# Two of six modulation vectors computed inside the recurrence instead of in the input stream

## The reference, cut to what matters

```python
def ada_modulation(cvec, w_mod, b_mod):
    m = jax.nn.silu(cvec) @ w_mod + b_mod          # (2 vectors, 2048) @ (2048, 6 * 2048)
    return jnp.split(m[:, None, :], N_MOD, axis=-1)

sh1, sc1, g1, sh2, sc2, g2 = ada_modulation(cvec, lp['w_mod'], lp['b_mod'])
h = rmsnorm(x, lp['n1']) * (1.0 + sc1) + sh1
(q, k, v, glu_a, glu_b, r, kc, vc, ...) = split_columns(h @ lp['w_in'])
# attention (q, k, v), convolution module (glu_a, glu_b), two-way RWKV-7 recurrence (r, kc, vc, ...)
y = jnp.concatenate([y_a, y_b, y_c], axis=-1) @ lp['w_out']
x = x + g1 * y
h2 = rmsnorm(x, lp['n2']) * (1.0 + sc2) + sh2
x = x + g2 * conv_ffn(h2, lp['w_up'], lp['ffn_conv_w'], lp['ffn_conv_b'], lp['w_down'])
```

## Time and profile before

| | us |
|---|---|
| median of 3 runs | 2195.0 (2190.41 to 2195.76) |
| the profiled execution, its own time | 2199.24 |
| its span | 2197.5 |
| PE busy in it | 2081.4 |
| DVE busy | 1042.3 |
| ACT busy | 725.4 |

### The profile page before, as it was taken

One profiled execution on the slowest core, in us unless ns is written; L12 is line 12 of the kernel. 1 busy time (PEld: TensorE's weight loads), 2 busy tenths in 40 slices (PEclk: granted clock), 3 DMA queues, 4 the chain that ended last, 5 costly groups with the idle time before them and its releaser, 6 DMA issues.

```text
span 2197.5 us, 43948 instructions
## 1 busy us (share of the span) xinstructions
PE 2081.4 (95%) x19367; PEld 1828.7 (83%) x19367; DVE 1042.3 (47%) x1821; ACT 725.4 (33%) x1224; POOL 169.5 (8%) x275
## 2 busy tenths in 40 slices
PE   6999999999888899899799999999999999999997
PEld 3578888777567787778699999999999998887886
DVE  2333223664657777543644444444443444445444
ACT  3231222222554444323433223333223333333433
POOL 1000000000325444200000000000000000000000
PEclk8999999999889999999899999999999999999999
DMA  9988767775310000163343343333434336333431
GB/s 370 370 289 295 291 250 276 279 267 201 97 31 9 18 16 14 61 267 115 134 135 127 122 135 117 133 127 123 134 117 132 129 121 249 126 124 115 134 134 58
DMA packets 204847, 343.01 MB, mean 156 GB/s; under 512 B 14782, under 2 KB 138484, under 8 KB 202545
## 3 DMA queue, kind: packets, MB, share of 16 engines
q1 hardware_dynamic: 203264, 335.15, 43.9%
q0 software_dynamic: 1392, 5.05, 0.7%
HBM read 332.62 MB, written 10.31 MB: 156 GB/s over the span
## 4 chain that ended last, share of the span: by engine, by line
PE 85%; DVE 8%; DMA 3%; issue 2%; POOL 1%; ACT 1%; SPq 0%; DVEq 0%; POOLq 0%; ACTq 0%
PE ps L812 25%; PE ps L814 24%; PE ps L813 24%; PE ps L851 3%; DMA ring<-in_w_mod_dram 3%; PE ps L1056 1%; PE ps L1048 1%; PE ps L1050 1%; PE ps L1173 1%; PE ps L1066 1%; POOL w_mix L690 1%; PE ps L1137 0%; PE ps L1106 0%; PE ps L998 0%; DVE h_split L1744 0%
## 5 line engine op out<-in xcount | busy, mean ns | idle before, releaser
L1675 DVE TENSOR_TENSOR w_split<-ring,w_split 128x1024 fp32r<-128x1024 f32 x392 | 474.6, 1218 | 715.8 <-ACT w_split L1348 715.5
L1348 ACT ACTIVATE w_split<-ring 128x1024 fp32r<-128x1024 f32 x392 | 406.7, 1051 | 845.7 <-PE ps L814 572.8
L812 PE MATMUL ps<-h_split,w_split 128*128 128x384 f32 x1776 | 597.6, 336 | 3.8 <-DVE h_split L2092 3.8
L813 PE MATMUL ps<-h_split,w_split 128*128 128x384 f32 x1776 | 594.5, 335 | 0.0
L814 PE MATMUL ps<-h_split,w_split 128*128 128x384 f32 x1776 | 594.4, 335 | 0.0
L812 PEld LDWEIGHTS ps<-h_split,w_split 128*128 128x128 f32 x1776 | 334.1, 188 | 14.9 <-issue 13.6
L813 PEld LDWEIGHTS ps<-h_split,w_split 128*128 128x128 f32 x1776 | 334.2, 188 | 0.0
L814 PEld LDWEIGHTS ps<-h_split,w_split 128*128 128x128 f32 x1776 | 334.2, 188 | 0.0
L812 PE MATMUL ps<-w_split,h_split 128*128 128x512 f32 (+1 forms) x528 | 201.7, 382 | 2.2 <-DVE w_split L1675 2.0
L813 PE MATMUL ps<-w_split,h_split 128*128 128x512 f32 (+1 forms) x528 | 197.4, 374 | 0.0
L814 PE MATMUL ps<-w_split,h_split 128*128 128x512 f32 (+1 forms) x528 | 197.4, 374 | 0.0
(11 more groups left out here) (370 smaller groups left out, 2503.5 us busy)
## 6 DMA issues: line engine op xcount, KB each, us to landing
ring<-in_w_up_dram SPq DMA_DIRECT2D x88, 1024.0 KB, 4.9
ring<-in_w_mod_dram SPq DMA_DIRECT2D x64, 1024.0 KB, 7.4
ring<-in_w_in_dram SPq DMA_DIRECT2D x46, 1024.0 KB, 5.4
ring<-in_w_down_dram SPq DMA_DIRECT2D x44, 1024.0 KB, 5.3
ring<-in_w_mod_dram SPq DMA_DIRECT2D x64, 512.0 KB, 7.0
ring<-in_w_out_dram SPq DMA_DIRECT2D x16, 1024.0 KB, 5.5
arena<-in_x_sample_dram SPq DMA_DIRECT2D x4, 1024.0 KB, 9.1
x_mid<-arena SPq DMA_DIRECT2D x1, 3072.0 KB, 10.0
```

The costliest lines, as they stand in the source:

```text
L812: mm(o_, lh, rh, start=start, stop=False)
L813: mm(o_, lh, rl, start=False, stop=False)
L1348: AC(wh[k % SPLITS][:, 0:width(n)], arrived(n), ACT.Copy).then_inc(s_hi, 1)
L1675: V.tensor_tensor(wl[k % SPLITS][:, 0:w], arrived(n), wh[k % SPLITS][:, 0:w].bitcast(F32), ALU.subtract).then_inc(s_lo, 1)
```

## The change

The stream keeps only sh2 and sc2 behind the early blocks: 4 late blocks instead of 8, so 32 pieces of 1 MB leave it. The gates' 32 MB come as 128 loads of 256 KB (one K-tile by 512 columns) into four slots in `h_f32`, of which only two are used from load 72 on. PE multiplies one such tile ("gate step", four products side by side in 128 columns each) ahead of steps that `gate_fill` names: 8 steps in each of the periods -1 to 14. A burst of 8 steps adds up in the upper half of bank 7; ACT copies it to `gpart`, POOL adds the two bursts of a block, SP writes the sum to DRAM. The gates' bias enters as one more product. F2's tile moves to the lower half of bank 7.

```diff
-N_MOD = 6 * D // MOD_W
+N_LATE = 2 * D // MOD_W
+N_MOD = 2 * D // MOD_W + N_LATE
+LATE_COL = N_LATE // 2
...
+GATE_W = 4 * P
+N_GATE = 2 * D // GATE_W
+GATE_STEPS = N_GATE * KT
+GATE_BANK = 7
+def gate_fill(u, step):
+    if u < 0:
+        return dict(cum=4, tr=4).get(step, 0)
+    if u == 0:
+        return dict(X0=2, lora=1, X1=1, T1=2, X2=2).get(step, 0)
+    return dict(ZU=2, lora=1, X1=1, T1=2, S0=2).get(step, 0)
+GATE_BURST = KT // 2
+def gate_done(u):
+    return sum(1 for w in GATE_PLAN if w <= u)
+GATE_WIDE = gate_done(NG + 1) // 4 * 4
+def gate_slot(n):
+    return n % 4 if n < GATE_WIDE else 2 + n % 2
...
+        gslot = [hf[:, TOK * k:TOK * k + GATE_W] for k in (12, KT + 12)]
+        gslot += [hf[:, TOK * k - GATE_W:TOK * k] for k in (KT, 2 * KT)]
+        gpart, grow = (hf[:, TOK * k:TOK * k + 2 * P].rearrange("p (i c) -> p i c", i=2) for k in (14, KT + 14))
@@ SP
+            def gate_loads(upto):
+                for n in range(gates_at[0], min(upto, GATE_STEPS)):
+                    i, q = divmod(n, KT)
+                    if i and q == KT // 2:
+                        gate_out(i - 1)
+                        gates_at[1] = i
+                    earlier = [m for m in range(n) if gate_slot(m) == gate_slot(n)]
+                    if earlier:
+                        sp.wait_ge(s_gu, earlier[-1] + 1)
...
+                    sp.dma_start(gslot[gate_slot(n)], a["w_mod"][0][P * q:P * q + P, c0:c0 + GATE_W]).then_inc(s_w[gate_slot(n)], 16)
             sp.wait_ge(s_blk, P_OUT)
+            gate_loads(4)
             bias_rows(sp, 1)
...
             for gr in range(GROUPS):
+                gate_loads(gate_done(NG * gr + 2))
                 sp.wait_ge(s_stc, gr + 1)
...
                 if gr == 0:
+                    gate_loads(gate_done(NG + 1))
                     sp.wait_ge(s_rbon, NG)
                     sp.wait_ge(s_rlora, NG)
                     sp.wait_ge(s_fy, 3)
                     sp.wait_ge(s_fg, 3)
                     for i in range(3):
                         if i:
+                            gate_loads(gate_done(NG + 1 + i))
                             sp.wait_ge(s_rlora, NG + 3 + i)
                         params(2, range(3 * i, 3 * i + 3))
                 if gr == 1:
+                    gate_loads(GATE_STEPS)
+                    for i in range(gates_at[1], N_GATE):
+                        gate_out(i)
@@ POOL
-            pool.wait_ge(s_grow, 1)
-            for i in range(2):
-                for g in range(2):
-                    pool.dma_start(G_dram[i, g].rearrange("(k p) -> k p", p=P), grow[g:2 * KT:2, i, :]).then_inc(s_G, 16)
...
+                if u >= 0 and u % 2 == 0 and u < 2 * N_GATE:
+                    i = u // 2
+                    pool.wait_ge(s_gev, 2 * i + 2)
...
+                    pool_tt(grow[:, i % 2, :], gpart[:, 0, :], gpart[:, 1, :], ALU.add).then_inc(s_gsum, 1)
@@ PE
-            for i, c0 in enumerate((2 * KT, 5 * KT)):
-                last = tr(ps[0:2 * KT, 4, toks(i)], modcol[:, c0:c0 + KT, :].rearrange("p k g -> p (k g)"), ident)
-            last.then_inc(s_gT, 1)
+            own_bank = dict(F1=0, F2=0, out=0)
+            own_bank["in"] = 0
+            def gate_step(k):
+                for n in range(gates_at[0], min(gates_at[0] + k, GATE_STEPS)):
...
+                    first = n % GATE_BURST == 0
+                    if first and n:
+                        pe.wait_ge(s_gev, n // GATE_BURST)
+                    for taken, count in ((s_fc, own_bank["F2"]), (s_stc, own_bank["out"]), (s_S0, 2 * own_bank["in"])):
+                        if count:
+                            pe.wait_ge(taken, count)
+                    pe.wait_ge(s_w[gate_slot(n)], gate_landed(n))
+                    at = [ps[32 * g:32 * g + 2, GATE_BANK, HW:HW + P] for g in range(MG)]
+                    if q == 0:
+                        for g in range(MG):
+                            mm(at[g], modcol[:, tile + g, :], ident, start=True, stop=False)
+                    for g in range(MG):
+                        last = mm(at[g], c2_t[:, 2 * q:2 * q + 2], gslot[gate_slot(n)][:, toks(g)], start=(first and q > 0), stop=((n + 1) % GATE_BURST == 0))
+                    last.then_inc(s_gu, 1)
...
                 for step, v in steps(ORDER_PE, u):
+                    gate_step(gate_fill(u, step))
+                    if step in own_bank:
+                        if gates_at[0] >= GATE_BURST:
+                            pe.wait_ge(s_gev, gates_at[0] // GATE_BURST)
+                        own_bank[step] += 1
                     rwkv_step(u, step, v)
@@ ACT
+            def gate_rows(b):
+                ac.wait_ge(s_gu, GATE_BURST * (b + 1))
...
+                AC(gpart[:, b % 2, :], ps[:, GATE_BANK, HW:HW + P], ACT.Copy).then_inc(s_gev, 1)
...
+                    if step[0] == "X2" and u + 1 < 2 * N_GATE:
+                        gate_rows(u + 1)
```

More of the change, by code:

```diff
@@ L215 @@
 PERIODS = range(-1, NU + 2)
+GATE_W = 4 * P
[9 more added lines that the diff above has]
+GATE_BURST = KT // 2
+GATE_PLAN = [u for u in PERIODS for step, _v in steps(ORDER_PE, u) for _ in range(gate_fill(u, step))]
+GATE_PLAN = GATE_PLAN[:GATE_STEPS]
+assert GATE_PLAN == [n // GATE_BURST - 1 for n in range(GATE_STEPS)]
+def gate_done(u):
[3 more added lines that the diff above has]
+    return n % 4 if n < GATE_WIDE else 2 + n % 2
 def unit(v):
@@ L424, in build @@
         s_blk, s_kd = sem("s_blk"), sem("s_kd")
-        s_ah, s_al, s_c4, s_hm, s_hh, s_xs, s_x3 = (sem(n) for n in ("s_ah", "s_al", "s_c4", "s_hm", "s_hh", "s_xs", "s_x3"))
+        s_ah, s_al, s_c4, s_hm, s_hh, s_xs = (sem(n) for n in ("s_ah", "s_al", "s_c4", "s_hm", "s_hh", "s_xs"))
         s_cs, s_cyh, s_pvh, s_fh, s_hms, s_hmp, s_hh2 = (sem(n) for n in (
@@ L495, in landed, with gate_landed @@
         def landed(n):
-            return 16 * sum(cuts(m) for m in range(n % RING, n + 1, RING))
+            gates = sum(1 for m in range(GATE_STEPS) if gate_slot(m) == n % RING) if 2 * n >= P_OUT else 0
+            return 16 * (gates + sum(cuts(m) for m in range(n % RING, n + 1, RING)))
+        def gate_landed(n):
+            return landed(P_OUT // 2 - RING + gate_slot(n)) + 16 * sum(1 for m in range(n + 1) if gate_slot(m) == gate_slot(n))
         def used(eng, n):
@@ L555, in _ @@
                 elif kind == "mod":
-                    load(n, a["w_mod"][0][rows, MOD_W * i:MOD_W * (i + 1)].rearrange("(k p) c -> p k c", p=P), MOD_KP)
+                    cs = slice(MOD_W * (i + LATE_COL), MOD_W * (i + LATE_COL + 1))
+                    load(n, a["w_mod"][0][rows, cs].rearrange("(k p) c -> p k c", p=P), MOD_KP)
                 else:
@@ L580, in states, with gate_out @@
                                  src.rearrange("h v k -> v h k")).then_inc(s_sraw, 16)
+            gates_at = [0, 0]
+            def gate_out(i):
+                sp.wait_ge(s_gsum, i + 1)
+                if i % (N_GATE // 2):
+                    sp.wait_ge(s_G if i < N_GATE // 2 else s_G2, 32 * (i % (N_GATE // 2)))
+                for b in range(2):
+                    dst = G_dram[i // (N_GATE // 2), b, GATE_W * (i % (N_GATE // 2)):GATE_W * (i % (N_GATE // 2) + 1)]
+                    sp.dma_start(dst.rearrange("(g c) -> g c", c=P), grow[b:P:32, i % 2, :]).then_inc(s_G if i < N_GATE // 2 else s_G2, 16)
+            def gate_loads(upto):
[7 more added lines that the diff above has]
+                        sp.wait_ge(s_gu, earlier[-1] + 1)
+                    c0 = (2 if i < N_GATE // 2 else 4) * D + GATE_W * i
+                    c0 -= 0 if i < N_GATE // 2 else GATE_W * (N_GATE // 2) - D
+                    sp.dma_start(gslot[gate_slot(n)], a["w_mod"][0][P * q:P * q + P, c0:c0 + GATE_W]).then_inc(s_w[gate_slot(n)], 16)
+                    gates_at[0] = n + 1
             sp.wait_ge(s_blk, P_OUT)
-            sp.wait_ge(s_E1, 32)
+            gate_loads(4)
+            sp.wait_ge(s_E1, 48)
             bias_rows(sp, 1)
@@ L1225, in rwkv_step @@
                     for i in range(CT):
-                        last = tr(ps[:, 7, toks(CT + i)], Oacc[t_][:, toks(i)], ident)
+                        last = tr(ps[:, 7, toks(i)], Oacc[t_][:, toks(i)], ident)
                     last.then_inc(s_fT, 1)
@@ L1536, in _ @@
                 for step in steps(ORDER_ACT, u):
+                    if u < 0 and step[0] == "tr":
+                        gate_rows(0)
+                    if step == ("F2", (GROUPS - 1) * NG + 1):
+                        ac.wait_ge(s_gsum, N_GATE)
                     rwkv_step(u, *step)
+                    if step[0] == "X2" and u + 1 < 2 * N_GATE:
+                        gate_rows(u + 1)
                     if step == ("tr", 0):
@@ L1755, in _ @@
                     lo(n)
+            for c0 in (2 * KT, 5 * KT):
+                V.tensor_copy(modcol[:, c0:c0 + KT, :], vcol[:, 0, 32 + c0:32 + c0 + KT].unsqueeze(2).broadcast_to([P, KT, 2]))
             dv.wait_ge(s_h, PAIRS)
```

47 lines of the change are left out of this document (26 added, 21 removed).

## The result

The changed kernel takes 2268.6 us (median of 4 runs, 2267.4 to 2274.6) against 2195.4 (2190.4 to 2201.3) for the kernel before in the same session: ratio 1.034 [1.032, 1.036], that is +73 us. The forecast was slower by 57.5 us, 2253, in a range of 2200 to 2285. Direction and range held; the point was 16 us low.

A forecast was written before the change was run, and what follows sets the result against it. PE was taken to bound the stream, and DVE's fixed chain from S0 the recurrence. Terms -30 + 24 + 7 + 43 + 11 + 2.5 gave +57.5 us, hence 2253 us, in a range of 2200 to 2285.

The forecast's parts named there:

- What bounds the kernel: PE bounds the input stream; in the recurrence DVE takes over from S0, so what delays S0 delays everything behind it.
- The stream, -30: Input stream: 32 `w_mod` pieces at 0.88 us and four column turns removed, 30 us less (bounds -28 and -33).
- PE's products, +24: Recurrence: six gate steps of 0.25 us at lora, X1, T1, S0 push S0 by 1.5 us a period: +24 (18 to 36).
- Four slots, +7: Periods 1 to 7: S0's second tile lands 1.05 us after PE asks for it: +7 us (5 to 16).
- two slots, +43: Periods 8 to 14: S0's tiles hang on T1's, 6.1 us of waiting each: +43 us (33 to 67).
- The shared bank, +11: Gate steps and ZU wait 1.9 us for DVE's last F2, after six periods: +11 us (6 to 12).
- SP's queue, +2.5: Tile 32, first of period 3, is issued behind period 2's `out` and `in` DMAs: +2.5 us (0 to 5).
- The sum: Whole kernel: -30 + 24 + 7 + 43 + 11 + 2.5 = +57.5 us, giving 2253 us.
- loads in time: Rival, chance 0.10: recurrence tiles are there when asked for, 50 us fall away: +7.5, 2202 us.
- faster: Rival, chance 0.17: tiles in time or waits off the path, products fill PE's idle 23.5 us: about -20, 2175 us.
- PE catches up: Rival, chance 0.13: waiting PE replaces the recurrence's 23.5 us of idle PE: +34, 2229 us.
- The clock falls as well: Rival, chance 0.12: stops in seven periods lower PE's clock, slowing steps ahead of S0: +19 more, 2272 us.

The follow-up runs named there:

- experiment 1: Kernel before with only the 32 gate pieces and their turns taken out of the input stream, gates holding their bias alone: 2157.1 us, ratio 0.984.
- experiment 2: Changed kernel with only the first four gate tiles loaded and reused; all products, bank waits and copies kept: 2199.7 us, ratio 1.003 to before.
- experiment 5: Experiment 3 with SP issuing gate tiles ahead of the parameters and four tiles further ahead: 2232.0 us, ratio 1.016 to before.
- experiment 3: Changed kernel with four slots to the end, two of them in free stretches of `consts` from load 72 on: 2248.1 us, ratio 1.025 to before.
- experiment 7: Experiment 5 with four of the six gate steps ahead of X1, T1 and S0 moved behind S0: 2222.0 us, ratio 1.011 to before.
- experiment 9: Experiment 8 with only six of its 128 gate tiles loaded, products unchanged: 2190.6 us, ratio 0.998 to before.
- experiment 6: Experiment 5 with the two gate steps ahead of ZU moved ahead of lora in the six periods behind an F2: 2221.2 us, ratio 1.012 to before.
- experiment 8: Experiment 7 with no gate steps ahead of ZU in the six periods behind an F2, as in experiment 6: 2217.5 us, ratio 1.010 to before.
- experiment 11: Experiment 1 plus the 128 loads of 256 KB in the recurrence, which nothing uses: 2171.0 us, ratio 0.990 to before.
- experiment 10: Experiment 8 with 120 of its 128 loads cut from 256 KB to 16 KB, same number of DMAs: 2191.8 us, ratio 0.999 to before.

## Why the prediction was right, and where it was off

The parts are the stream -35.7 (experiment 1), products, bank and copies +42.6 (experiment 2 less 1), and loads +68.9 (after less experiment 2). Their sum is 75.8, against 73.2 for after less before; the 2.6 us between them is the difference of the kernel before in the two sessions. Of the loads' 69, experiment 5 gives 16 to their place in SP's queue and experiment 3 gives 20.5 to the two slots. The other 32 hold the waits with four slots, the lower clock and what traffic costs; no experiment parts them.

- **What bounds the kernel.** Right for the stream: taking PE work out shortened it by a little more than the work. Half right for the recurrence: S0's place rules, but "from S0 on DVE takes over" was too clean. Experiment 7 shows that PE's steps behind S0 cost nearly as much as those ahead of it. Without loads it is the same: experiment 9, with the late places and no wait for F2, is 9 us faster than experiment 2, and the wait for F2 alone was 10.8 in experiment 6.
- **The stream, -30.** Right in kind, measured -35.7. A piece and its turn gave 1.04 us instead of 0.93 (3.4 us over 32), 1.8 us came at the start (the prediction left 3 us of PE's early idle time out), and 1.3 us were a wait ahead of the last turn. Why a piece gives more than the 0.88 that the chain shows stays open.
- **PE's products, +24.** Mis-sized: 42.6 less the bank's 10.8 leaves 32, within the bounds of 18 to 36; ACT's copies and POOL's sums, costed at nothing, are in it. The prediction let two steps per period go for nothing in the gap ahead of ZU, which it read from periods 5 and 6 (0.91 and 0.45 us). Its own row of period 4 has 0.21, and over the periods 1 to 14 the gap is 0.3 us on average, 4.4 us in all, against 7 for the two steps. The clock is in the 32 as well: 0.95 in experiment 2 and 0.99 in experiment 1.
- **Four slots, +7, and two slots, +43.** The walk from slot to tile gave S0 at 13.0 us behind ZU in periods 8 to 14; the trace's mean is 12.8. Before it was 6.2 on average, not the 5.4 of period 5, so S0 came 6.6 us later and not 7.6. PE's idle time put down to tiles in these periods sums to 28 us. As a cause it was right and the largest single one; as a price, 36 for two slots in place of four was too high: experiment 3 gave back 20.5. The load's time of 3.1 us was right (3.0). The formula that the prediction took for comparison from "DMA: Bandwidth & Descriptors" of the Trainium skill stands there for DMAs of GpSimd's queue, and these are SP's.
- **The shared bank, +11.** Measured 10.8, right to the decimal by luck (the same cure gave 4.5 between experiments 7 and 8), but the mechanism (PE queued behind DVE's L2039) is the one removed in experiment 6.
- **SP's queue, +2.5.** A term that was missed nearly whole. The prediction looked at tile 32 behind the states, and forgot `params` of the second group, which stand in the queue between tiles 0 to 3 and tile 4. Experiment 5 gave 16 us.
- **No term for traffic or for the clock.** The prediction cost a load only by when it lands. Added to a kernel that doesn't use them, the same loads cost 13.9 us (experiment 11), though DMA was idle for 95% of that stage. In after the stops they cause elsewhere don't show (10.9 us against 10.0 without loads), so no run gives a figure for traffic in after. The clock was a rival with a price, and its price was no part of the sum.
- **The sum.** 57.5 became 73 to 76. The stream gained 6 more than predicted; products (+8) and SP's queue (+13) cost more. What is left of the loads is 53 us, against 50 for the slots. In it the waits for slots cost less than predicted, and the lower clock, which was in no term, fills the gap. So the point came within 16 us partly by luck.

The rivals: **loads in time** and **faster** need tiles in under some 1.2 us; they land in 3.0. Even with every tile there (experiment 2) the kernel isn't faster than before, and with the best places for the steps too (experiment 9) it only draws level, within 0.2%. **PE catches up** would have been 2229; PE's time outside its busy time grew by 13 and 28 us instead. **The clock falls as well** was given 0.12 and is the rival that the record bears out in good part. Its 2272 is nearer to the measured 2268.6 than the forecast's 2253. Between the ZUs of periods 1 and 15 the mean granted clock is 0.91 over 314 us in after and 0.98 over 220 us before. An estimate from this: 27 and 5 us of full-speed time are missing, so the clock cost up to 22 us where the rival had 19. PE's busy time for the same matmuls says the same, 250.5 us in after against 226.9 at a clock of 1.00 (experiment 10). It is an upper bound, as not all of this time is on the path, and no experiment changed the clock alone. With four slots throughout the clock was 0.92 and 0.91, with two throughout 0.87 in either half: the more PE waits, the lower it is.

## What to carry to other kernels

In this kernel an engine that is busy for 90% of a loop had no room for a filler in any of the places tried: work whose removal from the stream gave 36 us cost 32 in the recurrence with every load in time. When a load is tied to a slot, count the steps from a slot's use to its next use against the time from issue to landing (here 3.2 us at the median: four slots nearly do, two don't), and walk the whole issuing queue from the first load on, since a block of 13 unrelated DMAs in it delayed a load by 6.5 us. Price the clock together with every wait of the engine. And an idle DMA wasn't free to use: price the bytes against the engine that runs through many small instructions at the same time.

## What the runs showed of the hardware that was not expected

- Loads that nobody waits for slow PE: 128 of 256 KB in some 230 us cost 13.9 us (experiment 11). Part of it are stops of 0.4 to 2.3 us in front of matmuls without a wait, part is longer busy time at a lower clock (0.96 against 0.99). With 120 loads cut to 16 KB the time was within 1.2 us of that without loads.
- PE gets its instructions in packets of 16384 bytes, 256 recorded instructions each, and stands when one is late: every stop in the traces of experiments 8 and 11 ends 1.15 to 1.65 us after the end of such a packet. The kernel before has 11 such stops too, 9.5 us in its recurrence. Small matmuls run through a block in as little as 3.0 us.
- Fillers keep the clock where the kernel before lost it. The stretch from attention's end to the ZU of period 1, in before, experiment 1, experiment 2 and after:

```profile
625.00:650.90 25.90, 19.30 (x418) 15.60 (x418) 9.88 (x28) 15.33 (x30) 9.36 (x18) 0.67 0.24 63
589.00:614.30 25.30, 19.02 (x416) 15.32 (x408) 9.59 (x27) 15.35 (x30) 9.08 (x18) 0.66 0.27 64
589.00:611.50 22.50, 19.03 (x578) 13.66 (x578) 10.07 (x29) 15.67 (x32) 9.60 (x19) 1.00 0.23 73
589.00:624.30 35.30, 22.79 (x580) 15.09 (x576) 10.37 (x29) 16.17 (x33) 9.49 (x19) 0.81 0.52 166
```

  The granted clock is 0.67 and 0.66 without fillers (1.2 GHz for much of it), 1.00 with them and no waits for loads, and 0.81 with waits. "TensorE: Matmul & The Clock Gate" of the Trainium skill, in its part on the HAM clock gate, lets the clock follow how busy PE has lately been. The first three rows agree. The fourth has a higher clock than the first at a smaller busy share of its stretch, so the share over a whole stretch doesn't tell the clock. The gain lies within the 42.6 and wasn't measured by itself.
- 256 KB land in 3.0 us after issue in after (median of 128; 2.5 at least). The 64 KB of the states took 2.7 in the kernel before and 3.2 in after. In experiment 11 the median is 3.9; there a load waits for its slot's last one to land but not for any product, so that up to four are in flight at once.
